# Routed expert rows added straight into the two outputs of a decoder step, with an eight-row add for the decode rows and a new order of GpSimd's gathers

## The reference

```python
x = x + (ga * y_a + gb * y_b) @ w_out
x = x + moe(rmsnorm(x, norm2_g), ...)

def moe(h, ...):                       # h: tokens x 1024
    eidx, gw = route(hf, w_router, router_bias)      # top 8 of 64 experts
    routed = routed_experts(hf, eidx, gw, ...)       # SwiGLU 1024 -> 256 -> 1024 each, weighted, summed
    shared = swiglu(hf, w_s_gate, w_s_up, w_s_down)
    return routed + shared
```

## Time and profile before

| | us |
|---|---|
| median of 3 runs | 2171.42 |
| lowest, highest | 2160.67, 2175.79 |
| the profiled execution's own time | 2168.33 |
| its span, first to last instruction | 2166.4 |

### The profile page before, as it was taken

How to read it: one execution, slowest core, us unless ns; L and a number is a source line. 1 busy time by engine, 2 the same in 40 slices (tenths; PEclk the granted TensorE clock), 3 DMA queues, 4 the chain that set the end, 5 groups by cost and what they waited for, 6 DMA issues and landing times. The chain is left out here.

```text
span 2166.4 us, 37247 instructions
## 1 busy us (share of the span) xinstructions
PE 1990.3 (92%) x12464; PEld 1501.9 (69%) x12464; DVE 1323.1 (61%) x2267; ACT 1033.7 (48%) x1542; POOL 846.1 (39%) x788
## 2 busy tenths in 40 slices
PE   7999889969799999999989888999999999999994
PEld 5777767747444448888868644777777777777773
DVE  4388767666676663111157644777777777777772
ACT  6322213357566663111034212667666667676772
POOL 2111123333577751110004651454646555445442
PEclk9999989979899999999999999999999999999997
DMA  7488821055655565885072416899999999999995
GB/s 232 146 270 262 263 96 40 18 161 183 202 161 163 166 210 184 291 281 184 20 250 88 147 40 240 299 356 351 351 331 359 337 348 344 352 348 357 347 352 137
DMA packets 172368, 501.95 MB, mean 232 GB/s; under 512 B 26327, under 2 KB 73774, under 8 KB 145822
## 3 DMA queue, kind: packets, MB, share of 16 engines
q1 hardware_dynamic: 130070, 355.43, 45.4%
q0 software_dynamic: 31200, 79.17, 14.5%
q10 hardware_dynamic: 10992, 66.02, 9.0%
HBM read 438.01 MB, written 120.75 MB: 258 GB/s over the span
## 5 line engine op out<-in xcount | busy, mean ns | idle before, releaser
L2795 DVE TENSOR_TENSOR w_gu_lo<-turned,w_gu_hi 128x2048 fp32r<-128x2048 f32 x132 | 302.7, 2294 | 105.0 <-ACT w_gu_hi L2709 101.4
L2709 ACT ACTIVATE w_gu_hi<-turned 128x2048 fp32r<-128x2048 f32 x132 | 252.6, 1915 | 43.3 <-PEq L1957 43.3
L2557 POOL DMA_INDIRECT x_scratch<-turned,target x66 | 126.8, 1921 | 321.4 <-DMA x_scratch<-turned,target 282.5
L647 PE MATMUL pP<-wring,hT_hi 128*128 128x512 f32 (+1 forms) x576 | 226.2, 393 | 19.7 <-DVE wring L573 12.9
L649 PE MATMUL pP<-wring,hT_lo 128*128 128x512 f32 (+1 forms) x576 | 221.5, 385 | 0.0
L648 PE MATMUL pP<-wring,hT_hi 128*128 128x512 f32 (+1 forms) x576 | 221.0, 384 | 0.0
L2632 PE MATMUL pG_e<-w_gu_hi,xT_hi 128*128 128x512 f32 x528 | 217.3, 411 | 0.0
L2632 PE MATMUL pG_e<-w_gu_lo,xT_hi 128*128 128x512 f32 x528 | 210.2, 398 | 0.0
L2632 PE MATMUL pG_e<-w_gu_hi,xT_lo 128*128 128x512 f32 x528 | 209.9, 397 | 0.0
L2818 DVE TENSOR_TENSOR w_e_lo<-turned,w_e_hi 128x2048 fp32r<-128x2048 f32 x66 | 151.1, 2290 | 20.8 <-ACT w_e_hi L2723 20.8
L405 POOL TENSOR_TENSOR wring<-turned,wring 128x512 fp32r<-128x512 f32 (+1 forms) x43 | 67.4, 1592 | 228.9 <-ACT wring L439 228.7
(11 more groups left out here) (355 smaller groups left out, 4736.8 us busy)
## 6 DMA issues: line engine op xcount, KB each, us to landing
turned<-in_w_e_up SPq DMA_DIRECT2D x65, 1024.0 KB
turned<-in_w_e_down SPq DMA_DIRECT2D x65, 1024.0 KB
turned<-in_cache_sb_kv SPq DMA_DIRECT2D x256, 256.0 KB, 3.1
turned<-in_w_e_gate SPq DMA_DIRECT2D x64, 1024.0 KB
out<-in_cache_win_kv ACTq DMA_DIRECT2D x8, 4094.0 KB
turned<-in_w_in ACTq DMA_DIRECT2D x56, 256.0 KB, 6.5
turned<-in_w_in SPq DMA_DIRECT2D x16, 512.0 KB, 7.7
out<-in_cache_win_kv ACTq DMA_DIRECT2D x8, 1022.0 KB
```

The lines of the kernel that those rows point to most:

```text
L647: pe.matmul(pP[:m, i % 4, :w], hi, w_hi(u), start=(c == 0), stop=False)
L2557: pool.indirect_dma_start(sc["x2"], bass.IndirectOffsetOnAxis(ap=target[:, j, 0:1], axis=0), y[j], None, bounds_check=T - 1, oob_is_err=Fa ...
L2709: act.activation(ghi[:, r, k, :, :].rearrange("p c f -> p (c f)"), w[:, r, k, :], ACT.Copy).then_inc(ghi_ready, 1)
L2795: dve.tensor_tensor(glo[:, r, k, :, :].rearrange("p c f -> p (c f)"), w[:, r, k, :], ghi[:, r, k, :, :].rearrange("p c f -> p (c f)").bitc ...
```

## The change

The scratch tensor `x2` goes, with its fill of 160 zero rows and the copies at the end. The phase before stores x into the outputs (eight tiles to y_prompt, the decode tile to y_sample). Each add becomes an add to y_prompt, whose bound now leaves out the decode rows (S = 1024 in place of T), and right behind it an add of the place's first eight slots to y_sample, through a new table `samp_row` (row number less 1024 for a decode row, out of bounds for any other) and a new copy of it in `aim`. `y_out` therefore counts 80 a turn in place of 48. GpSimd's turn becomes: aim long, add long, aim short, gather short, gather the next turn's long rows, add short. `gT` moves to the bank of `pQ`, with a wait for ScalarE's copy of the turn before, and VectorE copies `hid_tail` ahead of hid_lo. The number of turns stays the same; `load_last` is rewritten for the new loop bounds. The core of the diff:

```diff
@@ phase_out_route @@
-                sp.dma_start(sc["x2"][T:, :].rearrange("(p n) d -> p n d", n=5), zero...).then_inc(zero_out, 16)
...
-                    sp.dma_start(sc["x2"][t * P:t * P + m, :], x2[:m, t % 2, :]).then_inc(x2_out[t % 2], 16)
+                    dst = o[0][0, t * P:t * P + m, :] if t < NT - 1 else o[1][:, 0]
+                    sp.dma_start(dst, x2[:m, t % 2, :]).then_inc(x2_out[t % 2], 16)
...
                 dve.tensor_copy(slot_info[:, :, 0], pT[:, :NBLK]).then_inc(slots_ready, 1)
+                chain(dve.tensor_scalar(samp_far[:, :], pT[:NS, :NBLK], float(S), float(8 * S), ALU.is_lt, ALU.mult))
+                chain(dve.scalar_tensor_tensor(samp_row[:, :], pT[:NS, :NBLK], -float(S), samp_far[:, :], ALU.add, ALU.add))
@@ phase_experts @@
-        gT = pH[:, NF * P:NF * P + NF * TAIL].rearrange("p (f t) -> p f t", f=NF)
+        gT = pQ[:, QW:QW + NF * TAIL].rearrange("p (f t) -> p f t", f=NF)
...
-                sp.wait_ge(y_out, last * 48 + 48)
-                sp.dma_start(o[1][:, 0], sc["x2"][S:T, :]).then_inc(copied, 16)
-                sp.dma_start(half_rows(o[0][0], 0), half_rows(sc["x2"], 0)).then_inc(copied, 16)
-                sp.wait_ge(copied, 48)
+                sp.wait_ge(y_out, last * 80 + 80)
+                sp.nop(nofuse=True)
...
                     pool.tensor_copy(target[:, j, :], slot_info[:, bass.ds(it * U + j, 1), :]).then_inc(target_ready, 1)
+                    pool.tensor_copy(samp_target[:, j:j + 1], samp_row[:, bass.ds(it * U + j, 1)]).then_inc(samp_target_ready, 1)
...
-                        pool.wait_ge(y_out, it * 48 + 32 * j)
+                        pool.wait_ge(y_out, it * 80 + 48 * j)
                     pool.wait_ge(y_copied, it * 3 + 2 * (j == SHORT) + 1)
...
-                    pool.indirect_dma_start(sc["x2"], bass.IndirectOffsetOnAxis(ap=target[:, j, 0:1], axis=0), y[j], None,
-                                            bounds_check=T - 1, oob_is_err=False, compute_op=ALU.add).then_inc(y_out, 16)
+                    pool.indirect_dma_start(y_rows, bass.IndirectOffsetOnAxis(ap=target[:, j, 0:1], axis=0), y[j], None,
+                                            bounds_check=S - 1, oob_is_err=False, compute_op=ALU.add).then_inc(y_out, 16)
+                    pool.indirect_dma_start(y_samp, bass.IndirectOffsetOnAxis(ap=samp_target[:, j:j + 1], axis=0), y[j][:NS], None,
+                                            bounds_check=NS - 1, oob_is_err=False, compute_op=ALU.add).then_inc(y_out, 16)
...
-                def body(it, old):
-                    for j in range(U):
-                        if old is not None:
-                            aim(old, j)
-                        if seen(it, j, 2):
-                            gather(it, j)
-                        if old is not None:
-                            scatter(old, j)
+                def body(it, old, final=False):
+                    aim(old, LONG)
+                    scatter(old, LONG)
+                    aim(old, SHORT)
+                    gather(it, SHORT)
+                    if not final:
+                        gather(it + 1, LONG)
+                    scatter(old, SHORT)
...
                     if j == LONG:
                         pe.wait_ge(hid_q_ready, it + 1)
+                        if seen(it, LONG, 1):
+                            pe.wait_ge(y_copied, it * 3 - 1)
...
-                        act.wait_ge(y_out, it * 48 if j == SHORT else it * 48 - 16)
+                        act.wait_ge(y_out, it * 80 if j == SHORT else it * 80 - 32)
...
+                    if j == LONG:
+                        dve.wait_ge(hT_psum, it * U + 1)
+                        if seen(it, LONG, 1):
+                            dve.wait_ge(tail_done, it)
+                        dve.tensor_copy(hid_t[:, :, :], gT).then_inc(hid_t_ready, 1)
                     dve.wait_ge(hhi_ready, it * U + (j + 1))
...
-                    if j == LONG:
-                        dve.tensor_copy(hid_t[:, :, :], gT).then_inc(hid_t_ready, 1)
```

More of the change, by code:

```diff
@@ L177, in build @@
             branches.close()
-            phase_out_route(nc, a, o, scratch, ident, turned, expert_row, slot_info)
-            phase_experts(nc, a, o, scratch, ident, turned, expert_row, slot_info)
+            samp_row = attention.enter_context(nc.sbuf_tensor("samp_row", [NS, NBLK], I32))
+            phase_out_route(nc, a, o, scratch, ident, turned, expert_row, slot_info, samp_row)
+            phase_experts(nc, a, o, scratch, ident, turned, expert_row, slot_info, samp_row)
 def phase_project(nc, a, o, sc, ident, turned):
@@ L2294, in count_blocks @@
                     chain(dve.tensor_tensor(turns[:, :], turns[:, :], long_blocks, ALU.max))
-                    dve.tensor_scalar(expert_row[0:1, NBLK:], turns[0:1, :], -2.0, None, ALU.add).then_inc(row_ready, 1)
+                    dve.tensor_scalar(expert_row[0:1, NBLK:], turns[0:1, :], -3.0, None, ALU.add).then_inc(row_ready, 1)
                     half, kept, odd, block_no, past, short, first, own, key, held, unit, used, rest = (eb[:, c:c + 1] for c in range(13))
@@ L2561, in scatter @@
                         pool.nop(nofuse=True)
-                        pool.indirect_dma_start(x2_quarters, bass.IndirectOffsetOnAxis(ap=target[:, j, 1:2], axis=0), y_tail, None,
-                                                bounds_check=QT * T - 1, oob_is_err=False, compute_op=ALU.add).then_inc(y_out, 16)
-                def body(it, old):
-                    for j in range(U):
-                        if old is not None:
-                            aim(old, j)
-                        if seen(it, j, 2):
-                            gather(it, j)
-                        if old is not None:
-                            scatter(old, j)
-                for it in range(LAG):
-                    body(it, None)
+                        pool.indirect_dma_start(y_quarters, bass.IndirectOffsetOnAxis(ap=target[:, j, 1:2], axis=0), y_tail, None,
+                                                bounds_check=QT * S - 1, oob_is_err=False, compute_op=ALU.add).then_inc(y_out, 16)
+                def body(it, old, final=False):
[6 more added lines that the diff above has]
+                    scatter(old, SHORT)
+                gather(1, LONG)
+                gather(1, SHORT)
+                gather(LAG, LONG)
                 last = load_last(pool)
-                with pool.Fori(LAG, last + 1) as it:
+                with pool.Fori(LAG, last) as it:
                     body(it, it - LAG)
+                body(last, last - LAG, final=True)
                 for n in range(LAG):
@@ L2581, in _ @@
                         scatter(last - (LAG - 1 - n), j)
-                pool.wait_ge(y_out, last * 48 + 48)
+                pool.wait_ge(y_out, last * 80 + 80)
                 pool.nop(nofuse=True)
@@ L2783, in _ @@
                 put(last, SHORT)
-                act.wait_ge(y_out, last * 48 + 48)
-                act.dma_start(half_rows(o[0][0], 1), half_rows(sc["x2"], 1)).then_inc(copied, 16)
-                act.wait_ge(copied, 48)
             @block.vector
```

26 lines of the change are left out of this document (13 added, 13 removed).

## The result

The changed kernel takes 2260.6 us (median of three runs, 2257.32 to 2262.1) beside 2171.42 before: a ratio of 1.0418, 95% interval 1.0356 to 1.0481. It is slower by about 90 us, where I had forecast 2142 and a range that ended at 2165. The profiled execution took 2262.1 us with a span of 2260.3, so 93.9 us of span were added to the 2166.4 before.

A forecast was written before the change was run, and what follows sets the result against it. TensorE and DMA were taken as nearly full, with GpSimd's chain of adds as long as TensorE's turn. Terms -13.4, -9.5, -5.0 and nothing sum to -27.9: 2140.4, plus 1.5 carried, so 2142 us; range 2132 to 2165.

The forecast's parts named there:

- The copy at the end: After the loop: the copy from scratch to outputs goes, two eight-row adds come; 13.4 us less, bounds 12.0 to 15.2.
- The hole: TensorE's idle before the tail's down product shrinks from 0.62 to 0.28 us in 28 turns; 9.5 us less.
- The stalls: Loop turns lengthened by late gathered rows, 10.0 us in all: gathering long rows earlier removes half, 5.0 us.
- late next: The long place's index and weight copy, still behind the short adds; ScalarE had 2.9 us of waiting a turn to swallow more.
- The work added to the chain: Eight-row adds, small copies and the moved gather on GpSimd cost nothing, hidden by the adds' landings.
- The durations: GpSimd's work between long and short adds would take 11.6 us, an eight-row add 1.16 of it.
- The cover: Between long and short adds, 11.6 us of work against 12.53 in which adds land anyway: 0.9 us to spare.
- The order: The next long rows' gather, 3.47 us with its index copy and more, moves ahead of the short adds, under the landing.
- uncovered: Upper bound for GpSimd's added work if landings do not hide it: 2.7 us a turn.
- The rivals: Three other outcomes: everything comes true, 2136 us (0.22); the chain of adds keeps its pace, 2156 (0.25); slower, 2192 (0.10).
- slower: GpSimd's instructions between long and short adds outlast the 12.53 us landing, 1.16 us a turn: 2192 us, chance 0.10.

The follow-up runs named there:

- The run meant to test this: The changed kernel with the copies of the next long place's row numbers and weights moved ahead of the short place's adds: ratio 1.0789.
- the steps above: Kernels from before to after, adding one part each: copy gone 0.9947, the hole's edit 0.9945, GpSimd's new order 1.0144, eight-row adds 1.0418.
- fills: Kernel before plus three GpSimd fills of a spare tile a turn: 1.0003 right ahead of the short add, 1.0098 between the long place's 128-row and quarter-row adds.

## Why the prediction was wrong, point by point

**The copy at the end (-13.4).** The copy is gone and the size came out, in part by luck. From the last turn's row to the end it is 13.7 us less; by itself the edit gives 11.5. From the start of the last main add to the end I had 6.6 us and it is 10.4: from the end of the last eight-row add to the end of the span are 7.2 us, where I had a landing of 3.94; the DMA engines carry nothing from 2256 on. From the last turn's row to that add I had 33.4 us and it is 29.4. The two errors cancel.

**The hole (-9.5).** The mechanism was right: the wait is 7.6 us for 17.4. The sum was wrong: 0. "If TensorE still sets the turn" was its condition. Alone, the edit did shorten the undisturbed turn by 0.40 us, but it measured 1.0036, since more turns had to wait for gathered rows (25.4 us for 9.1). GpSimd could follow at 23.2 us in most turns and not in all, and what TensorE gained it lost in the others. In the changed kernel TensorE doesn't set the turn at all.

**The stalls (-5.0).** TensorE's waits for gathered rows went altogether, and in a loop that GpSimd sets this too is worth nothing. What I named as late next, the copy of weights behind the short adds, is what ScalarE then waited for (1.4 to 228.1 us). That wait is behind the chain and doesn't set its length: once in the loop did a main add wait for ScalarE. The run meant to test this moved the cost and left the wait.

**The work added to the chain (nothing).** This is the step that failed: it cost 3.5 us a turn, 109 us in 31 turns, of which the steps above give some 43 to the order and 59 to the eight-row adds. It failed in three places.

- *The durations.* I summed 11.6 us of GpSimd work against a landing of 12.53 and took durations of instructions that ran freely. In the turn shown it was 14.63, in the mean 16.27. The eight-row add had 0.86 + 0.30 from a plain DMA of eight rows; it holds GpSimd 1.34 at the least (the last row of after), 1.90 in the mean of its 66, and 2.62 in this turn: 1.8 us more than summed. The quarter gather had 1.04 and took 2.76: 1.7 more. These two are more than the 3.0 us between 11.6 and 14.63; some smaller items came out shorter.
- *The cover.* I took the landing, 12.53 us after the first long add, as fixed. An eight-row add ahead of the tail's add moves the last issue of the group, and a part of that moves the landing. I had this at the end of the span, where the first one delays the quarter add, and left it out in the loop. That the place counts is shown by two pairs of kernels: fills at 1.0003 in the wait and 1.0098 ahead of the tail's add, and eight-row adds that cost 31 us less once they stand in the waits. How much arrives differs: 1.5 of 2.6 us a turn for the eight-row adds, nothing in the mean link for the fills.
- *The order.* I counted the moved gather as work under a landing, with 0.9 us to spare. Alone the new order costs 43 to 48 us, and most of it isn't in the link that I added up: without eight-row adds long to short grew by 0.15 us a turn, and short to long by 1.49. There GpSimd has 3.5 us of work less, as I had it, and waits for the landing in 27 of 28 turns, and still the link is longer; but for the 0.7 us of the short add's own issue, why is open. With the eight-row adds on top, long to short has no waiting left at all (24 of 26 "issue"), and they add 1.95 us there. My bound of 2.7 us a turn for "uncovered" was too low as well: the loop lost 3.5.

**Why the durations were longer.** In the turn shown, these two rows of VectorE ran beside the quarter gather (2019.39 to 2022.15):

```profile
2018.98 2.29 DVE L2799 TENSOR_TENSOR w_gu_lo<-turned,w_gu_hi 128x2048 fp32r<-128x2048 f32 x1 [0.90 <-ACT w_gu_hi L2716]
...
2021.52 2.28 DVE L2799 TENSOR_TENSOR w_gu_lo<-turned,w_gu_hi 128x2048 fp32r<-128x2048 f32 x1
```

The gather starts 0.41 us behind the first and ends 0.88 behind its end, near the 1.04 that it takes when free. That looks like GpSimd held until VectorE is done, for DMA instructions as for copies, and the rows of all indirect DMAs in the loop say the same. Between 1380 and 2100, 146 of GpSimd's 208 indirect DMAs start while such a subtraction of 128x2048 runs, and last 1.06 us longer in the mean than the shortest of their line; of the other 62 none is more than 0.06 us above it, though a subtraction begins during some. The 25 held quarter gathers all end 0.87 to 0.89 us after the subtraction, the 47 held eight-row adds 1.20 to 1.26. Before, 61 of 180 start so. In the long-to-short link this lengthening is 4.72 us a turn, for 1.13 before, so 3.6 more, where the link grew by 2.8. The turn fell so that the quarter gather met such a row in nearly every turn (mean 2.71 us between 1400 and 2100, for 1.48 before).

The Trainium skill ("SBUF — State Buffer", section "Who interferes with whom") states the exclusion that I had weighed and set aside, for a VectorE instruction with two SBUF inputs beside a GpSimd instruction that reads SBUF. Of DMAs that GpSimd writes out, the same section says that such a `tensor_tensor` was not seen to stall one; the rows here show it in every case, and the measurement decides. I had argued that a stretch in one turn is slack in the next; with GpSimd occupied all along a link there is no slack. No run changed VectorE's work alone, so this cause is read from rows and not tested; why the changed kernel's turn puts so many issues beside a subtraction is open too.

**The rivals.** What came is the one that I called "slower" and gave 0.10: GpSimd's instructions between the long and the short adds outlast the landing, and the short adds say "issue". Its sign was named in advance. Its price, one uncovered eight-row add of 1.16 us a turn, was a third of the 3.5 measured, so 2192 was 69 us too low, and it leaves out what the order costs in the other link. I gave it little weight because each added instruction was cheap alone; the cover of 0.9 us on 12.53, on durations with a known spread of 0.18 to 2.39, should have given it the largest chance.

## What to carry to other kernels

In a chain of waits, write down each link as the engine's own work and the landing behind its last issue, and add to the work only what the trace shows for such instructions at that place and beside the same neighbours, not their free durations. An instruction that is free inside a wait can cost ahead of the issue that the wait is for: here the same instructions cost 21 and 31 us more there. Read each link over the whole loop and not in one turn: one turn put the order's cost in the wrong link here. Where one engine's turn is cut and the next has no room to follow in every turn, the cut can be worth nothing, and work added to the fuller one counts at once.

## What the runs showed of the hardware

- An indirect DMA with an add costs GpSimd nearly the same for eight rows (1.34 us at the end of the span, 1.90 mean) as for 128 (1.59 there, 2.26 mean): nearly all of the price is per instruction.
- The issue of an indirect DMA is stretched as a copy is: in the kernel after, each one that started during a VectorE subtraction of 128x2048 ended a fixed time after it (the quarter gather 0.87 to 0.89 us), and the others kept their free duration to within 0.06 us.
- A small copy of index data that an add waits for costs far more than its 0.2 us where it stands in the chain: two of them took 4.06 us before the add could start.
